# Attention logits from stacked float32r parts, zero-padded values, and outputs gated where they are turned, in a two-block kernel

## The reference, cut to what matters

```
# family a (NSA), for each head, queries qa
s = qa @ kc.T * 64**-0.5 - slope*dist     # 31 compressed keys
s = qa @ ks.T * 64**-0.5 - slope*dist     # selected keys: with 512 tokens all blocks, causal
s = qa @ kw.T * 64**-0.5 - slope*dist     # window 512: causal
o_a = g0*softmax(..)@vc + g1*softmax(..)@vs + g2*softmax(..)@vw
y_a = (merge(o_a) * silu(z_a)) @ w_o_nsa
# family b (SWA), window 128, one more logit ("sink") per head
o_b = softmax([qb @ kb.T * 64**-0.5 - slope*dist, sink])[..., :-1] @ vb
y_b = (merge(o_b) * silu(z_b)) @ w_o_swa
y = (sigmoid(m_a) * y_a + sigmoid(m_b) * y_b) @ w_out
```

## Time and profile before

| | us or share |
|---|---|
| median of three runs | 1727.71 |
| profiled execution, device time | 1728.46 |
| its span, first to last instruction | 1726.7 |
| TensorE matmuls busy | 1636.3 (95%) |
| TensorE weight loads busy | 1415.2 (82%) |
| VectorE / ScalarE / GpSimd busy | 750.3 / 536.5 / 606.0 |
| mean granted TensorE clock | 0.968 |
| chain that ended last, by engine | issue 40%, PE 37%, POOL 17%, DVE 4% |

### The profile page before, as it was taken

How to read it: one execution, slowest core, us unless ns; L and a number is a source line. 1 busy time by engine, 2 the same in 40 slices (tenths; PEclk the granted TensorE clock), 3 DMA queues, 4 the chain that set the end, 5 groups by cost and what they waited for, 6 DMA issues and landing times.

```text
span 1726.7 us, 25059 instructions
## 1 busy us (share of the span) xinstructions
PE 1636.3 (95%) x9782; PEld 1415.2 (82%) x9782; DVE 750.3 (43%) x1489; ACT 536.5 (31%) x842; POOL 606.0 (35%) x485
## 2 busy tenths in 40 slices
PE   5898999999989989999999999989999999999996
PEld 5676777777767789999999999978788778878885
DVE  5705455554565753333233321232632462262255
ACT  2332333233332343222332222232332342233232
POOL 3454212222215423344434344233243244324332
PEclk9999999999989969999999999989999999999998
DMA  8132111111113401222222222222122122112111
GB/s 330 73 115 81 50 49 49 49 49 49 49 73 116 176 25 74 96 97 90 80 83 87 97 82 89 73 74 74 49 80 76 63 73 93 53 51 95 73 49 73
DMA packets 22738, 140.56 MB, mean 81 GB/s; under 512 B 3248, under 2 KB 3248, under 8 KB 6448
## 3 DMA queue, kind: packets, MB, share of 16 engines
q1 hardware_dynamic: 18752, 131.08, 20.6%
q10 hardware_dynamic: 3952, 9.00, 1.4%
HBM read 137.98 MB, written 2.10 MB: 81 GB/s over the span
## 4 chain that ended last, share of the span: by engine, by line
issue 40%; PE 37%; POOL 17%; DVE 4%; ACT 1%; POOLq 0%; DVEq 0%; ACTq 0%
PE lin L365 31%; POOL w_lo L311 17%; PE aux L788 3%; PE aux L760 1%; DVE mix L1466 1%; PE aux L746 1%; ACT w_hi L353 0%; PE aux L442 0%; DVE squares L1484 0%; PE aux L399 0%; PE aux L716 0%; PE aux L748 0%; DVE tmp L1405 0%; DVE residual L1509 0%; ACT mix L1019 0%
## 5 line engine op out<-in xcount | busy, mean ns | idle before, releaser
L311 POOL TENSOR_TENSOR w_lo<-w_raw,w_hi 128x512 fp32r<-128x512 f32 x460 | 602.3, 1341 | 1102.2 <-ACT w_hi L353 1102.2
L365 PE MATMUL lin<-x_hi,w_hi 128*128 128x272 f32 (+1 forms) x2128 | 590.6, 331 | 24.3 <-POOL w_lo L311 17.0
L365 PE MATMUL lin<-x_lo,w_hi 128*128 128x272 f32 (+1 forms) x2128 | 579.4, 326 | 0.0
L365 PE MATMUL lin<-x_hi,w_lo 128*128 128x272 f32 (+1 forms) x2128 | 578.1, 326 | 0.0
L365 PEld LDWEIGHTS lin<-x_hi,w_hi 128*128 128x128 f32 x2128 | 358.7, 192 | 71.1 <-issue 18.2
L365 PEld LDWEIGHTS lin<-x_hi,w_lo 128*128 128x128 f32 x2128 | 358.1, 192 | 32.5
L365 PEld LDWEIGHTS lin<-x_lo,w_hi 128*128 128x128 f32 x2128 | 358.6, 192 | 28.0
L353 ACT ACTIVATE w_hi<-w_raw 128x2048 fp32r<-128x2048 f32 x115 | 219.4, 1909 | 162.1 <-PE lin L365 156.6
L860 ACT ACTIVATE prob<-prob,neg_max 128x31 f32<-128x31 f32 (+6 forms) x128 | 60.1, 471 | 157.5 <-DVE neg_max L1196 157.5
L1317 DVE TENSOR_TENSOR conv_in<-conv_c_gate,lin 128x272 f32<-128x272 f32 (+1 forms) x32 | 12.3, 427 | 213.8 <-PE lin L365 213.8
L365 PE MATMUL lin<-mix,w_hi 128*128 128x512 f32 x256 | 81.9, 401 | 10.6 <-DVE mix L1466 7.1
(11 more groups left out here) (293 smaller groups left out, 1924.4 us busy)
## 6 DMA issues: line engine op xcount, KB each, us to landing
w_raw<-wstream SPq DMA_DIRECT2D x115, 1024.0 KB, 4.8
ada_shift_scale<-w_ada SPq DMA_DIRECT2D x8, 1024.0 KB, 19.1
ada_gate<-w_ada_gate ACTq DMA_DIRECT2D x4, 1024.0 KB, 5.7
residual<-x_t SPq DMA_DIRECT2D x1, 2048.0 KB, 8.9
residual<-x_t ACTq DMA_DIRECT2D x1, 2048.0 KB, 8.4
out_t<-residual ACTq DMA_DIRECT2D x8, 256.0 KB, 2.1
small_inputs<-smalls ACTq DMA_DIRECT2D x1, 537.0 KB, 3.5
residual<-meta_t ACTq DMA_DIRECT2D x1, 64.0 KB, 11.1
```

Of the source, the lines that this page charges most:

```text
L311: ins = eng.tensor_tensor(wlo[h][:, cols], raw[h][:, cols], whi[h][:, cols].bitcast(F32), ALU.subtract)
L365: ins = t.matmul(o, w[half][:, c0:c0 + P], x(k, t0, cnt), start=(n == 0), stop=(n == 3 * kts - 1))
```

## The change

Queries, the three kinds of keys and the compressed keys are kept as float32r high and low parts. `q_parts` holds a head's high part on its own 64 lanes and its low part on the other 64; `k_hi` and `k_lo` hold a head's parts twice, on both halves. So a logit is two float32r matmuls of 128 rows in place of one float32 matmul of 64 rows. ScalarE makes the high parts and VectorE the low parts, four instructions of 64 x 512 for a tile of keys, two for one of queries. The compressed keys get a 32nd zero column, the compressed values and turned probabilities zero rows up to 128. `scores(0)` of the next pair is issued at the end of a pair, before `turn_outputs(3)`, so the last pair is written out outside the loop. `outputs_turned` multiplies by z as it takes the tile out of PSUM, and the separate gating pass is gone; the output tiles of the first three pairs are then rounded first (`OG_ORDER`), and both halves of the first `w_o` chunk run tile by tile.

```diff
@@ TensorE
-                    eng.matmul(b[0][:, 0:keys], qa, proj[lo:hi, K_S, 0:keys], start=True, stop=True)
-                    eng.matmul(b[1][:, 0:keys], qa, proj[lo:hi, K_W, 0:keys], start=True, stop=True)
-                    eng.matmul(b[2][:, 0:NC], qa, kct[lo:hi, e * NC:(e + 1) * NC], start=True, stop=True)
...
+                if s == 0:
+                    eng.wait_ge(s_q, ii * 2 + 2)
...
+                for out, x, high, low in (
+                        (b[0][:, 0:keys], 0, k_hi[:, K_S, e, 0:keys], k_lo(K_S, e)[:, 0:keys]),
+                        (b[1][:, 0:keys], 0, k_hi[:, K_W, e, 0:keys], k_lo(K_W, e)[:, 0:keys]),
+                        (b[2][:, 0:NC + 1], 0, kct_hi[:, e, :], kct_lo[:, e, :]),
+                        (b[2][:, w0:w0 + keys - k0], 1, k_hi[:, K_B, e, k0:keys], k_lo(K_B, e)[:, k0:keys])):
+                    for part in (high, low):
+                        ins = eng.matmul(out, q_parts[:, x, e, qs], part, start=(part is high), stop=(part is low))
...
-                    eng.matmul(o[:, 0:DH], prob_T[0:NC, 1024:1152], vct[0:NC, e, :], start=True, stop=True)
+                    eng.matmul(o[:, 0:DH], prob_T[:, 1024:1152], vct[:, e, :], start=True, stop=True)
...
+                if not last:
+                    scores(0, ii + 1)
                 turn_outputs(QT - 1)
...
+            chunk_ready(START["wo"])
+            for n, k in enumerate(OG_ORDER):
+                eng.wait_ge(s_og_lo, n + 1)
+                for m in range(2):
+                    ins = wo_tile(0, m, k // 4, ks=[k % 4])
@@ ScalarE
+            def query_high_parts(g):
+                for e, (p0, p1) in enumerate(PAIR):
+                    ins = act(q_parts[p0:p1, g, e, :], lin[g][p0:p1, 0, :], ACT.Copy, scale=DH ** -0.5)
+                ins.then_inc(s_qhi, 1)
...
+                if c in KEYS:
+                    eng.wait_ge(s_proj, PROJ_ORDER.index(c) + 1)
+                    for e, (p0, p1) in enumerate(PAIR):
+                        for half in range(2):
+                            ins = act(k_hi[half * DH:(half + 1) * DH, KEYS[c], e, :], lin[0][p0:p1, 0, :], ACT.Copy)
+                    ins.then_inc(s_khi, 1)
...
-            for k in range(KD):
-                eng.wait_ge(s_og, k + 1)
-                act(xhi[:, k, 0:T1], tmp[:, k % 2, 0:T1], ACT.Copy).then_inc(s_og_hi, 1)
+            eng.wait_ge(s_chunk, START["wo"])
+            for k in OG_ORDER:
+                x, pr = divmod(k, NPAIR)
+                eng.wait_ge(s_oT_out, 4 * (NPAIR if pr == NPAIR - 1 else NPAIR - 1) + CREDIT)
+                act(xhi[:, k, 0:T1], zz[:, x, pr, :], ACT.Copy).then_inc(s_og_hi, 1)
@@ VectorE
+            def query_low_parts(g, at):
+                eng.wait_ge(s_qhi, at)
+                for e, (p0, p1) in enumerate(PAIR):
+                    o0, o1 = PAIR[1 - e]
+                    ins = stt(q_parts[o0:o1, g, e, :], lin[g][p0:p1, 0, :], DH ** -0.5, q_parts[p0:p1, g, e, :].bitcast(F32),
+                              ALU.mult, ALU.subtract)
+                ins.then_inc(s_q, 1)
...
                     for x in range(2):
-                        ins = move(flat(proj[:, bass.ds(ii + Q_B * x, 1), P * i:P * i + P]), turn_bank(i)[:, P * x:P * x + P])
+                        z = flat(zz[:, x, bass.ds(ii, 1), P * i:P * i + P])
+                        ins = stt(z, z, 0.5, turn_bank(i)[:, P * x:P * x + P], ALU.mult, ALU.mult)
...
+                    if s >= 6:
+                        query_low_parts(s - 6, ii * 2 + (s - 3))
                     eng.wait_ge(s_pv, ii * 8 + (s + 1))
```

More of the change, by code:

```diff
@@ L163, in build @@
         tmp = sb("tmp", [2, T2])
+        stage_b = ExitStack()
+        sb("squares_used", [T2 + 272], stack=stage_b)
+        kct_hi, kct_lo = (sb(f"kc_T_{part}", [2, NC + 1], F32R, stage_b) for part in ("hi", "lo"))
+        stage_b.close()
         sq = sb("squares", [2, T2])
+        k_lo_b = sb("keys_lo_swa", [2, T2], F32R, stage_b)
+        stage_b.close()
         ssum = sb("square_sum", [T2])
@@ L469, in build, with k_lo @@
         U_COL = 300
+        def k_lo(t, e):
+            return k_lo_b[:, e, 0:T1] if t == K_B else k_lo_sw[:, t, e, :]
+        OG_ORDER = [k for k in range(KD) if k % NPAIR < NPAIR - 1] + [NPAIR - 1, KD - 1]
         CREDIT = 2
@@ L595, in turn_outputs, with pair @@
+            def pair(ii, last):
                 def turn_outputs(i):
@@ L626, in _ @@
                     if s + 1 < 2 * QT:
[L627 removed]
+                        scores(s + 1, ii)
                     group(eng, c % 2, g * P, 256, KD, lin_outs(g, TB1), x_hi, x_lo,
@@ L644, in _, with wo_tile @@
                         turn_outputs(i - 1)
+                if not last:
+                    scores(0, ii + 1)
                 turn_outputs(QT - 1)
-            eng.wait_ge(s_tile_out, 6 * NPAIR + CREDIT)
-            for c in range(N_WO):
+            scores(0, 0)
+            with eng.bass.Fori(0, NPAIR - 1, 1, engines=[eng.engine]) as ii:
+                pair(ii, False)
+            pair(NPAIR - 1, True)
+            eng.wait_ge(s_tile_out, 4 * NPAIR)
+            eng.wait_ge(s_q, 2 * NPAIR + 2)
+            def wo_tile(c, m, x, ks=None):
+                return group(eng, c % 2, x * 1024 + m * P, 256, 4, [(wo_bank(2 * c + m, x)[:], TB1[0])],
+                             lambda k, t0, n: x_hi(4 * x + k, t0, n), lambda k, t0, n: x_lo(4 * x + k, t0, n), ks)
+            chunk_ready(START["wo"])
[3 more added lines that the diff above has]
+                    ins = wo_tile(0, m, k // 4, ks=[k % 4])
+                    if k % 4 == 3:
+                        ins.then_inc(s_chunk if m and k == KD - 1 else s_wo, 1)
+            for c in range(1, N_WO):
                 chunk_ready(START["wo"] + c)
@@ L1136, in values_turned @@
                 eng.wait_ge(s_vt, s + 1)
-                copy(proj[:, V_TILES[s], :], v_banks[s][:, 0:T1]).then_inc(s_vt_out, 1)
+                copy(values[:, V_TILES[s], :], v_banks[s][:, 0:T1]).then_inc(s_vt_out, 1)
             def hidden(src):
@@ L1156, in _ @@
             hidden(0)
+            for g in range(2):
+                query_low_parts(g, g + 1)
             hidden_turned(0)
             eng.wait_ge(s_cmp, 1)
-            ts(kct[:], aux[1][:, 0:2 * NC], 0.5, None, ALU.mult).then_inc(s_cmp_out, 1)
+            kc_raw = aux[1][:, 0:2 * NC].rearrange("p (g j) -> p g j", g=2)
+            for part in (kct_hi, kct_lo):
+                own.up(ts(part[:, :, NC:NC + 1], ones[:, 0:2].unsqueeze(2), 0.0, None, ALU.mult))
+            own.up(ts(kct_hi[:, :, 0:NC], kc_raw, 0.5, None, ALU.mult))
+            own.settle()
+            stt(kct_lo[:, :, 0:NC], kc_raw, 0.5, kct_hi[:, :, 0:NC].bitcast(F32), ALU.mult, ALU.subtract).then_inc(s_cmp_out, 1)
             eng.wait_ge(s_gatesT, 1)
@@ L1166, in _ @@
             copy_out(8, lambda: hidden_turned(1))
+            for zero in (vct[:].rearrange("p g d -> p (g d)"), probs_T[0][:, 1024:1152], probs_T[1][:, 1024:1152]):
+                own.up(eng.memset(zero, 0.0))
+            own.settle()
             eng.wait_ge(s_cmp, 2)
```

121 lines of the change are left out of this document (62 added, 59 removed).

## The result

The changed kernel takes 1701.21 us (median of four runs, 1699.95 to 1702.93), the kernel before beside it 1727.55 (four runs, 1726.42 to 1729.01): ratio 0.9848, 95% interval 0.9836 to 0.986. The move is -26.3 us where -32.4 was forecast. The profiled execution took 1699.95 us, its span is 1698.2, 28.5 shorter than before; TensorE is busy 94% of it, at a mean clock of 0.970.

The account below looks back on a forecast made before the run. TensorE, busy 95% of the span, was taken as the bound. Inside pairs -35.6, borders +2.7, projections +4.1, after the last pair -3.4, last step 7 -0.2: -32.4 from 1728.46 gives 1696.1, median 1695; range 1684 to 1711.

Parts of the forecast that it names:

- Logits, heights, weighted sums: Attention steps inside pairs: shorter logits 6.1, logit height 1.2, weighted sums 1.6; 8.9 us gained a pair, 35.6 for four.
- Rival B: Weighted sums and logits: height of the weights is not what costs, padding gives nothing; 11.2 us less gain, 1706; chance 0.08.
- Softmax keeps up: Inside pairs: softmax stays ahead of TensorE with 1.8 us slack; copies for step 7 hidden with 0.3 us to spare.
- A: Late attention steps: softmax or the low parts become the bound; 1713 if half of the 35.6 is lost; chance 0.12.
- C: Attention steps: with logits halved the clock falls inside steps, slower; 1749 with all 32 steps; chance 0.04.
- The border: Between pairs: 3.3 us gained over three borders, 6.0 lost to the low clock; 2.7 us lost as a whole.
- From here nothing is shorter: Border, from VectorE taking out the turned tile through moves, maxima and exponentials: unchanged at 6.65 us.
- the forecast gain of 1.1: Border, second half of step 7's tile to turning of step 0: 13.5 us in place of 14.57.
- The low clock in the step behind: After each border: idle time brings the low clock onto following work, costing 2.0 us, bounds 0 and 3.4; three times 6.0.
- Projections: ScalarE's key copies delay chunk 1 by 0.9 and chunk 8 by 3.2: cost 4.1 us, up to 7 at low clock.
- The 0.9 of chunk 1: Projections, chunk 1: ScalarE's key copies come late, the split waits 0.9 us, passed through GpSimd to TensorE.
- After the last pair: End of the weighted sums to the second `w_o` chunk: 17.2 us in place of 20.6, gain 3.4.

Follow-up runs that it names:

- the two padding experiments: Changed kernel with the zero rows of the compressed values' weighted sum undone: 1710.57 us; kernel before with only those zero rows added: 1718.53 us.
- the filler experiment: Changed kernel plus 16 matmuls of 512 columns, result overwritten, in TensorE's idle time at each of the three borders between pairs: 1693.79 us.
- the late logits: Changed kernel with the next pair's step 0 logits issued behind the turning of the last outputs instead of before it: 1694.80 us.
- all three edits together: Changed kernel without VectorE's ten border moves, with next pair's logits behind the outputs' turning and chunk 8's tanh ahead of the key copies: 1681.03 us.

## Why the prediction was near, and where it was off

*Logits, heights, weighted sums.* Right in mechanism, a little small: 36.1 against 33.2 between T1 and T7. The logits of i = 3 take 1.46 against 1.39 (the first of the eight is 0.31 from the second, not 0.233), but the rest gives more. The two records fall to 0.16, not to 0.23. The 12 matmuls ahead of them lose all of their 0.19 (2.98 to 2.79), of which the forecast gave 0.10 to the height: 0.09 of it goes with the zero rows (2.98 to 2.89 when they are the only change), the other 0.10 with the new logits. Rival B was that zero rows give nothing; the 9.4 and 9.5 us of the two padding experiments refute it. The Trainium skill, "TensorE: Matmul & The Clock Gate", section "LDWEIGHTS (loading the stationary operand)", speaks of how long a load takes, and there the traces agree with it: 0.18 to 0.19 us with 31 rows and with 128. That padding then gains nothing, as the prediction took from it, does not follow: what the height changes here is when the load starts.

*Softmax keeps up.* Right: there is no TensorE wait for softmax inside a pair, in steps 1 to 6 the clock is 1.00 (rivals A and C don't occur). Only the copies for step 7 end late by 0.3: from its second half tile to the sums 3.1 us in place of 2.8.

*The border.* The step that failed is "From here nothing is shorter: ... 239.95 - 233.30 = 6.65 us". That stretch was taken as fixed, and it holds a gate move of 1.25 us that ends with a piece of GpSimd. The change lets VectorE come to its moves at 229.08, inside GpSimd's run (227.05 to 232.04); before, it came at 233.97, 0.7 us from the end of one piece, and met the last one, to 235.90: one move was held 0.49 us and one 1.25. Two moves are now held for a whole piece, and the stretch is 7.50. With sums and half tile 0.6 longer than taken and the hand-overs, the forecast gain of 1.1 is a loss of 0.5 a border. The low clock in the step behind was put at 2.0 and cost 2.3, 3.1 and 2.5, the 7.8 of the filler experiment. The idle time was forecast at 3.7 and is 4.6. So the prediction saw the idle time and the clock. It took the idle time too short since it did not open the moves; the 2.0 for the clock was its choice between 0 and 3.4.

*Projections.* 3.2 forecast for the wait in chunk 8, 3.34 found. That the sum is near, 4.9 against 4.1, is in part luck. The 0.9 of chunk 1 is there at 80 us (TensorE goes on at 80.59 in place of 80.15, though it was 0.4 early at 45 us), but is gone again at 100 us, since the low clock behind it lasts to 83.8 and not, as before, to 85.0; chunk 8 begins at 125.87 against 126.08. In its place a low clock fell on the tile behind the wait, which takes 1.4 us longer.

*After the last pair.* 4.7 against 3.6: 3.2 from the sums to the first `w_o` matmul, 3.3 forecast. From there to the second chunk it is 12.75 us (479.85 to 492.60) in place of 13.9. Most of that is the 0.7 for both tiles of the chunk ending together, which no row shows: the second chunk follows at 0.23 us. The low clock, to 483.2, takes about 0.3 less than the 2.0 given for it.

## What to carry to other kernels

Before counting a chain on VectorE as fixed, look in it for short instructions of unusual length and ask which engine's piece they end with; a change that moves the chain moves it against that piece. A stall on TensorE costs more than its length when the clock is low behind it: price the next step at both levels, and prefer an order that puts the low stretch where another engine sets the pace. Fill the height of stationary operands that stand next to dense matmuls; 97 rows of zeros were worth 9.5 us here.

## What the runs showed of the hardware

VectorE held by GpSimd. In the attention steps of the changed kernel every `coef<-coef,gates_pair` that started well within a piece of GpSimd's split (12 of 12) ended with that piece, in up to 1.24 us in place of 0.16:

```profile
L1297 DVE TENSOR_TENSOR coef<-coef,gates_pair 128x3 f32<-128x3 f32 x32 | 15.8, 494 | 1.1
```

So did each gate move of four columns; the moves of one column (9 of 9 starts), the copies, reductions and everything that reads PSUM went on at their own times, and so did the reciprocal of four columns, one input from SBUF (8 starts well within a piece, 0.16 us each). This agrees with the exclusive lock that the Trainium skill describes in "SBUF — State Buffer", section "SBUF: two separate sides", for VectorE operations with two SBUF inputs or in a two-port mode: moves of one column are spared with one input (0.14 us) and held with two (0.52 to 0.56 us). That a one-input move of four columns is held and a reciprocal of four is not fits the rule if only the move takes a two-port mode; no trace here shows the mode.

The clock follows more than idle time. It was low behind idle times of 4.6 us and high behind 0.9 and 1.2, but with the late logits it is also low at 394.0, right behind a wait of only 1.3 us and on narrow matmuls. In the kernel before it falls at a wait of 1.30 too, at 231.8 us, and with all three edits together waits of 1.2 us at three borders brought it at one of them alone. Which of the two, the wait or the narrow matmuls, brought it there was not tried apart.
